# Light experts of a hierarchical MoE decoder layer: gate sums stored in block order, gated rows split on VectorE, list rows copied before the gather, the last expert gated by column halves

## The chip, the cores and the metric

The kernel runs on one core of a Trainium2 chip. The metric is the device time of one execution, in microseconds (us).

## The reference

One decoder layer over 1024 positions of width 1024 in float32. The first half is a mixer (gated linear attention for one group of columns, differential attention for another) with a residual sum. The second half, where the change lies, is a mixture of experts: each token picks one of 4 groups and in it 2 of 8 experts of width 512.

```python
def expert_block(args):
    xb, e = args
    hdn = jax.nn.silu(xb @ w1[e]) * (xb @ w3[e])
    return hdn @ w2[e]
...
out = jnp.zeros((n_tok + 1, d), f32).at[row_tok].add(y.astype(f32) * row_w[:, None])[:n_tok]
```

With 1024 tokens and 32 experts an expert has 64 rows in the mean.

## The kernel before

The part up to about 600 us computes the mixer and the router and puts the 32 experts in order of their row counts. From then on `over_experts` (L2404) runs the experts in that order, as loops written once per engine and unrolled by four: `pe_expert` (L2171), `act_expert` (L2220), `dve_expert` (L2299), `pool_expert` (L2385) and `sp_expert` (L2058). The engines run these streams in order and meet only at semaphores. The first 18 experts are heavy (HEAVY, up to CAP = 96 rows), the other 14 light (up to LIGHT_CAP = 64 rows). A last call with `tail=True` finishes the last expert.

**Weights.** An expert has six chunks of 1 MB: 0 and 1 of w1 (first gate), 2 and 3 of w2 (down), 4 and 5 of w3 (second gate). SP loads them two experts ahead, each when the low part of the same chunk two experts earlier is made (`load_chunk`, L1821; L1817 in the tail). Every chunk is split for fp32r products into a high part (`high`, L2042, a cast on ACT, 2048 columns) and a low part (`low`, L2046, raw minus high on DVE). The parts have three slots, chunk c in slot (c + 1) % 3, so `high` waits until PE has used the chunk three before (`chunk_used`), `low` waits for `high`, and PE waits for `low`.

**One expert on PE.** In the turn of expert e PE takes chunk 0, then brings the hidden part of expert e-1 into transposed form, takes chunk 1, transposes the gathered rows of expert e+1 (L1957), makes a token list (L1911), takes down chunks 2 and 3 of expert e-1, and chunks 4 and 5 of expert e. A heavy product is three matmuls of 512 columns (`product`, L2076 to L2078). A light expert puts the high part of its 64 rows in 64 columns of the weights and the low part in the other 64 (`xT_both`), so `gate` needs two matmuls (L2088, L2089), and the sums of the two halves stand in partitions 0 to 63 and 64 to 127 of PSUM.

**The fold.** These two halves have to be added and transposed. ACT copies each gate's sums to SBUF as `both[m]` (L2242 for the first gate, L2224 for the second, 512 columns), and `fold_mm` (L1968) multiplies them as weights with `fold`, two stacked unit matrices of 64: four matmuls of 64 columns for each gate, each recorded as two instructions, 16 in all. Hidden unit c*4 + k has to land at block k, so the loop reads every fourth column of `both` as weights; the tail, whose down weights are loaded in another row order (L1817), reads whole blocks:

```python
h = both[m][:, j * P:(j + 1) * P] if by_block else both[m].rearrange("p (c k) -> p k c", k=KE)[:, j, :]
last = nc.tensor.matmul(folded[m][:, j, :], h, fold[:], start=True, stop=True)
```

Behind the fold ACT applies SiLU (L2229, `slT`), DVE multiplies (L2294, `hT`), ACT casts the product to its high part (L2232, behind the high part of chunk 3), and DVE makes the low part (L2296), for which the down products wait (`hT_low`). In the tail all of it follows the last gate chunk: copy of 512 columns, both folds, SiLU, product, high, low, then `down_by_half` (L2122). Heavy experts use transposes instead (`h_transposes`, L1964), which read `hd` at the same stride of four.

**Rows in and out.** In each turn POOL first gathers the rows of expert e+3 (L1949, after the token list, L1922, is made), then copies the places and list rows of expert e+4 (`list_rows`, L2381 and L2382, about 1.9 us), for which DVE waits before its `pick` (L1903), and then scatters the rows of expert e-1 (L1990), which ACT has weighted (L2002).

Of the kernel before, what the change touches and what calls it, by code (L numbers as in the profile page):

```python
# [21 lines left out]
F32 = mybir.dt.float32  # L22
# [8 lines left out]
P = 128  # L31
# [1799 lines left out]
def stage_experts(nc, a, s, tools, front):  # L1831
# [44 lines left out]
    pt = four(banks["pt"])  # L1876
    py = [bank[0:CAP] for bank in banks["py"]]
    ph_both = banks["ph"]
    folded = [banks["pt"][:, 256 * m:256 * m + 256].rearrange("p (j x) -> p j x", j=KE) for m in range(2)]
    ident, rows, place, counts, iota = s["ident"], s["slot_rows"], s["place"], s["counts"], s["iota_slot"]  # L1880

# [142 lines left out]
    def slot(c, e=None):  # L2024
        if isinstance(e, int) and e == 0:
            return {0: 1, 1: 2, 4: 0, 5: 3}[c]
        return c + 2 if isinstance(e, int) and e == NE else (c + 1) % 3
# [94 lines left out]
    def down_by_half(pe, e):  # L2122

        for c in (2, 3):
            pe.wait_ge(w_low, number(e, c) + 1)
            for g in range(2):
                for k in range(KE // 2):
                    kx = KE // 2 * (c % 2) + k
                    w = slice(k * D + g * 512, k * D + g * 512 + 512)
                    last = product(py[g][:], hTh[:, kx, :], hTl[:, kx, :], wh[slot(c, e)][:, w],  # L2130
                                   wl[slot(c, e)][:, w], kx == 0, kx == KE - 1)
                if c == 3:
                    last.then_inc(chunk_used, 1)

    def list_tokens(pe, e):

# [34 lines left out]
    def pe_expert(pe, e, r, j, last, light, tail=False):  # L2171
        u = j % 2
        if isinstance(e, int) and e == 0:
            first_gate(pe)
            pe.wait_ge(xT_low, 2)
            gate(pe, 0, 1, u)
            list_weights(pe, 0)
            pe_x(pe, 1, 0, 1)
            list_weights(pe, 1)
            pe_ids(pe, 2, 0)  # L2180
            gate(pe, 0, 4, u)
            pe_ids(pe, 3, 1)
            gate(pe, 0, 5, u)
            return
        if not tail:
            pe.wait_ge(xT_low, 2 * e + 2)
            pe.wait_ge(q.silu, e)
            gate(pe, e, 0, u, light[1])
            if light[0]:
                if isinstance(e, int) and e == HEAVY + 1:  # L2190
                    pe.wait_ge(after["filled"], 13)
                pe.wait_ge(q.hd, e)
                fold_mm(pe, 0)
                fold_mm(pe, 1).then_inc(q.h_mm, 1)
# [24 lines left out]

    def act_expert(act, e, r, j, last, light, tail=False):  # L2220
        u = j % 2
        if light[0]:
            act.wait_ge(chunk_used, number(e - 1, 5) + 1)
            nc.scalar.copy(both[1][:], ph_both[1]).then_inc(q.hd, 1)  # L2224
        if some(e, 1) and not tail:
            high(act, e, r, u, 2)
        if light[0]:
# [5 lines left out]
        elif some(e, 1):  # L2233
            act.wait_ge(q.h_mm, e)
            nc.scalar.copy(hTh[:], pt[:]).then_inc(hT_high, 1)
            high(act, e, r, u, 3)
        if not tail:
            act.wait_ge(chunk_used, number(e, 1) + 1)
            if some(e, 1):
                act.wait_ge(q.hd, e)  # L2240
            if light[1]:
                nc.scalar.copy(both[0][:], ph_both[0]).then_inc(q.silu, 1)  # L2242
            else:
                silu(act, q)
            if some(e, 1):
                high(act, e, r, u, 4)
            if not (last and j == 3):
                act_x(act, e + 1, 1 - u, light[2])
            if some(e, 1):
                high(act, e, r, u, 5)  # L2250
            more = (0, 1) if not (last and j == 3) else ()
        else:
            more = ()
# [35 lines left out]
                nc.vector.tensor_tensor(xTl[u][:, k, :], px[g][:], xTh[u][:, k, :].bitcast(F32),  # L2289
                                        ALU.subtract).then_inc(xT_low, 1)  # L2290

    def turned_hidden(dve, e):
        dve.wait_ge(slT_ready, folds(e))
        nc.vector.tensor_tensor(hT[:], folded[1], slT[:], ALU.mult).then_inc(hT_ready, 1)  # L2294
        dve.wait_ge(hT_high, e)
        nc.vector.tensor_tensor(hTl[:, :, 0:LIGHT_CAP], hT[:], hTh[:, :, 0:LIGHT_CAP].bitcast(F32),  # L2296
                                ALU.subtract).then_inc(hT_low, 1)

    def dve_expert(dve, e, r, j, last, light, tail=False):  # L2299
        u = j % 2  # L2300
        if tail:
            turned_hidden(dve, e)
            low(dve, e, u, 3)
            return
        if light[0]:
# [354 lines left out]
```

## Time and profile before

| | us |
|---|---|
| median of three runs | 1220.89 (1220.45 to 1220.93) |
| profiled execution | 1221.63 |
| its span | 1219.80 |
| PE busy | 1157.8 |
| DVE busy | 882.8 |
| ACT busy | 697.8 |
| POOL busy | 329.5 |

The profile is that of one execution. Engines: PE is TensorE's matmuls, PEld its weight loads, DVE is VectorE, ACT is ScalarE, POOL is GpSimd, SP issues transfers. Times in the trace are counted from the start of the span. PEclk is the TensorE clock that was granted, as a share of full speed; the ends of matmuls are modelled, so starts are the better guide. PE's busy time can't tell how near a stage is to its limit, as an instruction that is loading or streaming slowly counts as busy.

### The profile page before, as it was taken

The numbers are of one execution on the slowest core, as the hardware profiler recorded it, in microseconds if no ns is written. First come the engines' busy times: TensorE is split into PE (matmuls) and PEld (weight loads), VectorE is DVE, ScalarE is ACT, GpSimd is POOL, SyncE is SP. The second block draws the span as 40 slices with busy tenths as digits, with TensorE's granted clock in tenths as the row PEclk, the third lists the DMA queues.
The fourth block names the chain that finished last, engine by engine and source line by source line (L and its number), as shares of the span: only waits on it lengthen the run. The fifth ranks groups of instructions, "written<-read, shape, count | busy, mean of one in ns | idle before, by whom it ended". The sixth has DMA issues, their size and how long they took to land.

```text
span 1219.8 us, 17253 instructions
## 1 busy us (share of the span) xinstructions
PE 1157.8 (95%) x5822; PEld 893.0 (73%) x5823; DVE 882.8 (72%) x1309; ACT 697.8 (57%) x943; POOL 329.5 (27%) x394
## 2 busy tenths in 40 slices
PE   6999999899999899997799999999999999999996
PEld 5868887677776678886567776777777878777774
DVE  4424324666577788886699899999999787888874
ACT  5424203554555633434367777777777676767773
POOL 2212103411111222224524334234243242424111
PEclk9999999999999999999799999999999898999998
DMA  8130210200200543445699999999999999999941
GB/s 315 39 104 1 104 69 1 76 29 27 95 27 19 174 165 134 131 156 207 236 368 389 385 375 395 382 371 390 373 376 386 365 366 341 335 350 340 343 151 18
DMA packets 67326, 271.65 MB, mean 223 GB/s; under 512 B 13172, under 2 KB 19896, under 8 KB 42808
## 3 DMA queue, kind: packets, MB, share of 16 engines
q1 hardware_dynamic: 57000, 245.32, 53.3%
q0 software_dynamic: 6800, 19.14, 6.8%
q10 hardware_dynamic: 3456, 6.29, 1.3%
q8 instruction: 39, 0.64, 0.2%
q14 instruction: 31, 0.25, 0.1%
HBM read 248.44 MB, written 26.48 MB: 225 GB/s over the span
## 4 chain that ended last, share of the span: by engine, by line
PE 80%; DVE 9%; ACT 4%; issue 3%; POOL 2%; DMA 1%; POOLq 0%; ACTq 0%; DVEq 0%
PE main_pm L693 12%; PE main_score L693 6%; PE main_score L2076 5%; PE main_score L2078 5%; PE main_score L2077 5%; PE main_score L1972 4%; DVE main_w_low L2046 3%; PE main_pt L2088 3%; PE main_score L754 3%; PE main_pt L2078 3%; PE main_pt L2076 3%; PE main_pt L2077 3%; PE main_po L2076 3%; PE main_po L2078 3%; PE main_po L2077 3%
## 5 line engine op out<-in xcount | busy, mean ns | idle before, releaser
L2046 DVE TENSOR_TENSOR main_w_low<-w_raw,main_w_high 128x2048 fp32r<-128x2048 f32 x190 | 433.7, 2290 | 39.1 <-ACT main_w_high L2042 38.6
L2042 ACT CAST main_w_high<-w_raw 128x2048 fp32r<-128x2048 f32 x190 | 362.2, 1908 | 72.8 <-PE main_score L2078 56.5
L1949 POOL DMA_INDIRECT main_xg<-xn_dram,main_token x32 | 70.7, 2210 | 359.7 <-DVE main_token L1922 351.8
L2076 PE MATMUL main_score<-main_w_high,main_hT_high 128*96 128x512 f32 x256 | 103.4, 404 | 4.7 <-DVE main_hT_low L2296 4.4
L2078 PE MATMUL main_score<-main_w_high,main_hT_low 128*96 128x512 f32 x256 | 101.2, 396 | 0.0
L2077 PE MATMUL main_score<-main_w_low,main_hT_high 128*96 128x512 f32 x256 | 101.0, 395 | 0.0
L693 PE MATMUL main_pm<-slot_high,xh 128*128 128x512 f32 x208 | 87.7, 422 | 2.1 <-DVE slot_low L1404 2.1
L693 PE MATMUL main_pm<-slot_low,xh 128*128 128x512 f32 x208 | 83.3, 400 | 0.0
L693 PE MATMUL main_pm<-slot_high,xl 128*128 128x512 f32 x208 | 83.0, 399 | 0.0
L1990 POOL DMA_INDIRECT out<-main_y,main_dest x31 | 64.8, 2089 | 57.8 <-ACT main_y L2002 53.4
L1055 ACT ACTIVATE main_prob<-main_score,main_nmax 128x128 f32<-128x128 f32 (+7 forms) x64 | 47.5, 743 | 33.5 <-DVE main_nmax L1463 32.7
L2088 PE MATMUL main_pt<-main_w_high,main_xT_both 128*128 128x512 f32 x112 | 52.6, 470 | 7.9 <-DVE main_w_low L2046 7.9
L2078 PE MATMUL main_po<-main_w_high,main_xT_low 128*96 128x512 f32 x144 | 57.9, 402 | 0.0
L2076 PE MATMUL main_po<-main_w_high,main_xT_high 128*96 128x512 f32 x144 | 57.7, 401 | 0.0
L2077 PE MATMUL main_po<-main_w_low,main_xT_high 128*96 128x512 f32 x144 | 57.6, 400 | 0.0
L2076 PEld LDWEIGHTS main_score<-main_w_high,main_hT_high 128*96 128x96 f32 x256 | 41.8, 163 | 21.2 <-DVE main_hT_low L2296 5.2
L2076 PE MATMUL main_pt<-main_w_high,main_xT_high 128*96 128x512 f32 x140 | 56.3, 402 | 0.0
L2078 PE MATMUL main_pt<-main_w_high,main_xT_low 128*96 128x512 f32 x140 | 55.4, 396 | 0.0
L2381 POOL COPY main_place_of<-place 128x8 f32 x30 | 55.0, 1834 | 1.5 <-POOL slot_rows L546 1.0
L2077 PE MATMUL main_pt<-main_w_low,main_xT_high 128*96 128x512 f32 x140 | 55.0, 393 | 0.0
L2078 PEld LDWEIGHTS main_score<-main_w_high,main_hT_low 128*96 128x96 f32 x256 | 41.7, 163 | 18.1
L2077 PEld LDWEIGHTS main_score<-main_w_low,main_hT_high 128*96 128x96 f32 x256 | 41.8, 163 | 15.8 <-issue 0.2
(359 smaller groups left out, 2627.4 us busy)
## 6 DMA issues: line engine op xcount, KB each, us to landing
w_raw<-in_moe_w SPq DMA_DIRECT2D x192, 1024.0 KB, 13.5
slot_raw<-in_w_in SPq DMA_DIRECT2D x12, 1024.0 KB, 7.6
main_x<-in_x SPq DMA_DIRECT2D x8, 512.0 KB, 11.6
slot_raw<-in_w_out SPq DMA_DIRECT2D x4, 1024.0 KB, 6.9
main_hx<-in_x SPq DMA_DIRECT2D x8, 512.0 KB, 4.0
out<-main_hx SPq DMA_DIRECT2D x8, 512.0 KB, 2.7
xn_dram<-main_xn SPq DMA_DIRECT2D x8, 512.0 KB, 2.9
gr_dram<-main_stage ACTq DMA_DIRECT2D x8, 256.0 KB, 2.0
```

The source lines that it names most:

```text
L693: last = nc.tensor.matmul(bank(i), stationary, moving, start=(k == 0 and n == 0), stop=(k == KD - 1 and n == 2))
L1055: nc.scalar.activation(out, score[comp][:, 0:nk], ACT.Exp, bias=nmax[:, n % 2, comp:comp + 1], accum_out=sums[:, n % 3, comp:comp + 1]).th ...
L1949: nc.gpsimd.indirect_dma_start(xg[u][:], None, s["xn2_dram"], bass.IndirectOffsetOnAxis(token[u][:, 0:1], 0), bounds_check=bound["x"], oob ...
L1972: last = nc.tensor.matmul(folded[m][:, j, :], h, fold[:], start=True, stop=True)
L1990: nc.gpsimd.indirect_dma_start(a["out"].rearrange("b n d -> (b n) d"), bass.IndirectOffsetOnAxis(dest[v][0:slots, 0:1], 0), y[u][0:slots], ...
L2042: nc.scalar.copy(wh[slot(c, e)][:], raw[u][c // 2][:, c % 2, :]).then_inc(w_high, 1)
L2046: nc.vector.tensor_tensor(wl[slot(c, e)][:], raw[u][c // 2][:, c % 2, :], wh[slot(c, e)][:].bitcast(F32), ALU.subtract).then_inc(w_low, 1)
L2076: nc.tensor.matmul(out, x_hi, w_hi, start=start, stop=False)
L2077: nc.tensor.matmul(out, x_hi, w_lo, start=False, stop=False)
L2078: return nc.tensor.matmul(out, x_lo, w_hi, start=False, stop=stop)
L2088: nc.tensor.matmul(ph_both[c // 4], xTb[u][:, kx, :], w_hi[:, w], start=(kx == 0), stop=False)
L2381: nc.gpsimd.tensor_copy(place_of[u][:], place[:, bass.ds(which, 1), :].rearrange("p a t -> p (a t)"))
```

## The change

Five things are changed; loads, loop structure and all other products stay.

1. In the loop ACT writes `both[m]` in block order, reading every fourth column of PSUM (`unfolded`), and `fold_mm` reads whole blocks always.
2. The high part of a light expert's gated rows is made by DVE, right behind the product, and not by ACT.
3. POOL copies the list rows of expert e+4 before the gather of expert e+3.
4. For the last expert PE folds the first gate before chunk 4, takes chunks 4 and 5 in halves of 256 columns into two PSUM banks (`gate_by_half`), and copy, fold, product, high and low part follow for each half.
5. In the tail the first down chunk waits for the first half of the hidden part alone, the second for the other (`down_by_half`).

```diff
-    def fold_mm(pe, m, by_block=False):
+    def fold_mm(pe, m, js=range(KE), out=None):
-        for j in range(KE):
-            h = both[m][:, j * P:(j + 1) * P] if by_block else both[m].rearrange("p (c k) -> p k c", k=KE)[:, j, :]
-            last = nc.tensor.matmul(folded[m][:, j, :], h, fold[:], start=True, stop=True)
+        for i, j in enumerate(js):
+            last = nc.tensor.matmul(folded[m][:, j, :] if out is None else out[:, i, :], both[m][:, j * P:(j + 1) * P],
+                                    fold[:], start=True, stop=True)
         return last
+    def unfolded(act, m):
+        return nc.scalar.copy(both[m].rearrange("p (k c) -> p k c", k=KE),
+                              ph_both[m].rearrange("p (c k) -> p k c", k=KE))
...
+    def gate_by_half(pe, e, u):
+        for c in (4, 5):
             pe.wait_ge(w_low, number(e, c) + 1)
+            w_hi, w_lo = wh[slot(c, e)], wl[slot(c, e)]
+            for half in range(2):
+                out = gated[half][:, 256 * half:256 * half + 256]
+                for k in range(KD // 2):
+                    w = slice(k * DE + 256 * half, k * DE + 256 * half + 256)
+                    kx = KD // 2 * (c % 2) + k
+                    nc.tensor.matmul(out, xTb[u][:, kx, :], w_hi[:, w], start=(kx == 0), stop=False)
+                    last = nc.tensor.matmul(out, xTb[u][:, kx, :], w_lo[:, w], start=False, stop=(kx == KD - 1))
+                if c == 5:
                     last.then_inc(chunk_used, 1)
+    def down_by_half(pe, e, c):
+        pe.wait_ge(hT_low, NE + c - 2)
+        pe.wait_ge(w_low, number(e, c) + 1)
...
-            gate(pe, e, 4, u, light[1])
-            gate(pe, e, 5, u, light[1])
+            if last and j == 3:
+                pe.wait_ge(q.silu, NE)
+                fold_mm(pe, 0).then_inc(q.h_mm, 1)
+                gate_by_half(pe, e, u)
+            else:
+                gate(pe, e, 4, u, light[1])
+                gate(pe, e, 5, u, light[1])
         else:
-            pe.wait_ge(q.hd, e)
-            fold_mm(pe, 0, by_block=True)
-            fold_mm(pe, 1, by_block=True).then_inc(q.h_mm, 1)
-            pe.wait_ge(hT_low, e)
+            for half in range(2):
+                pe.wait_ge(q.hd, NE + half)
+                fold_mm(pe, 1, (2 * half, 2 * half + 1), folded_half[half]).then_inc(q.h_mm, 1)
             pe.wait_ge(q.y_ready, 2 * e - 2)
-            down_by_half(pe, e)
+            for c in (2, 3):
+                down_by_half(pe, e, c)
...
     def act_expert(act, e, r, j, last, light, tail=False):
         u = j % 2
-        if light[0]:
+        if tail:
+            act.wait_ge(q.h_mm, NE)
+            nc.scalar.activation(slT[:], folded[0], ACT.Silu).then_inc(slT_ready, 1)
+            for half in range(2):
+                cols = slice(256 * half, 256 * half + 256)
+                act.wait_ge(chunk_used, number(e - 1, 4 + half) + 1)
+                nc.scalar.copy(both[1][:, cols], gated[half][:, cols]).then_inc(q.hd, 1)
+            high(act, e, r, u, 3)
+        elif light[0]:
             act.wait_ge(chunk_used, number(e - 1, 5) + 1)
-            nc.scalar.copy(both[1][:], ph_both[1]).then_inc(q.hd, 1)
+            unfolded(act, 1).then_inc(q.hd, 1)
...
             high(act, e, r, u, 3)
-            act.wait_ge(hT_ready, folds(e))
-            nc.scalar.copy(hTh[:, :, 0:LIGHT_CAP], hT[:]).then_inc(hT_high, 1)
...
-    def turned_hidden(dve, e):
+    def turned_hidden(dve, e, half=None):
+        k = slice(0, KE) if half is None else slice(2 * half, 2 * half + 2)
+        n = half or 0
+        if half is not None:
+            dve.wait_ge(q.h_mm, NE + 1 + half)
         dve.wait_ge(slT_ready, folds(e))
...
+        dve.wait_ge(hT_ready, folds(e) + n)
+        nc.vector.tensor_copy(hTh[:, k, 0:LIGHT_CAP], hT[:, k, :]).then_inc(hT_high, 1)
...
     def pool_expert(pool, e, r, j, last, light, tail=False):
         u = j % 2
+        if not last:
+            list_rows(pool, e + 4, u)
         if not (tail or (last and j >= 1)):
             pool_gather(pool, e + 3, 1 - u)
-        if not last:
-            list_rows(pool, e + 4, u)
```

## Rows read from the trace of the kernel before

**Rows 1.** the page, busy time of each engine over the span

```profile
PE 1157.8 (95%) x5822; PEld 893.0 (73%) x5823; DVE 882.8 (72%) x1309; ACT 697.8 (57%) x943; POOL 329.5 (27%) x394
```

**Rows 2.** stretches: length, busy of PE, PEld, DVE, ACT, POOL, PEclk, DMA share, GB/s

```profile
640.00:658.70 18.70, 18.66 (x94) 13.34 (x93) 16.93 (x16) 14.13 (x13) 6.49 (x4) 1.00 1.02 382
946.39:966.50 20.11, 19.46 (x90) 15.72 (x89) 16.42 (x16) 14.44 (x15) 6.76 (x5) 0.92 1.00 369
1066.20:1085.23 19.03, 18.45 (x89) 14.75 (x89) 16.30 (x16) 14.37 (x15) 6.29 (x5) 1.00 0.98 350
1010.30:1013.60 3.30, 3.30 (x9) 2.50 (x10) 1.04 (x4) 2.47 (x3) 0.00 (x0) 0.55 1.04 365
1069.70:1071.60 1.90, 1.90 (x9) 1.61 (x10) 0.52 (x2) 1.65 (x2) 0.00 (x0) 1.00 1.05 289
1183.30:1186.80 3.50, 3.50 (x17) 3.50 (x17) 3.16 (x2) 0.83 (x1) 0.00 (x0) 1.00 0.30 56
946.39:1183.30 236.91, 228.88 (x1040) 183.69 (x1040) 193.96 (x173) 173.08 (x169) 67.26 (x41) 0.94 0.93 331
```

**Rows 3.** timeline of PE in one light expert: start, length, engine, line

```profile
1066.20 3.72 PE L1972 MATMUL main_score<-main_fold,main_both 128*128 128x64 f32 x16
1069.72 0.48 PE L2088 MATMUL main_pt<-main_w_high,main_xT_both 128*128 128x512 f32 x1
...
1073.11 0.47 PE L2076 MATMUL main_score<-main_w_high,main_hT_high 128*96 128x512 f32 x1
...
1078.73 0.39 PE L2088 MATMUL main_po<-main_w_high,main_xT_both 128*128 128x512 f32 x1
...
1083.28 0.50 PE L2088 MATMUL main_pt<-main_w_high,main_xT_both 128*128 128x512 f32 x1 [0.44 <-DVE main_w_low L2046]
...
1085.23 1.15 PE L1972 MATMUL main_score<-main_fold,main_both 128*128 128x64 f32 x5
```

**Rows 4.** waits from 620 us on

```profile
PE main_pt L2088 <- DVE main_w_low L2046: 7.9, 13, 0.8
...
DVE main_onehot L1903 <- POOL main_rows_of L2382: 6.6, 27, 0.2
```

**Rows 5.** groups of L1972: 946 to 1187 us, then 1200 to 1203 us

```profile
L1972 PEld LDWEIGHTS main_score<-main_fold,main_both 128*128 128x128 f32 x208 | 49.5, 327 | 0.5
...
L1972 PEld LDWEIGHTS main_score<-main_fold,main_both 128*128 128x128 f32 x16 | 1.9, 192 | 1.1 <-ACT main_both L2224 1.1
```

**Rows 6.** timelines of DVE and of ACT in the same light expert

```profile
1065.31 4.49 DVE L2046 TENSOR_TENSOR main_w_low<-w_raw,main_w_high 128x2048 fp32r<-128x2048 f32 x2
...
1072.46 0.43 DVE L2296 TENSOR_TENSOR main_hT_low<-main_hT,main_hT_high 128x256 fp32r<-128x256 f32 x1 [1.67 <-ACT main_hT_high L2232]
...
1080.88 2.35 DVE L2046 TENSOR_TENSOR main_w_low<-w_raw,main_w_high 128x2048 fp32r<-128x2048 f32 x1 [0.20 <-ACT main_w_high L2042]
...
1072.03 0.40 ACT L2232 CAST main_hT_high<-main_hT 128x256 fp32r<-128x256 f32 x1
...
1078.93 1.92 ACT L2042 CAST main_w_high<-w_raw 128x2048 fp32r<-128x2048 f32 x1 [0.86 <-PE main_score L2078]
...
1083.69 0.58 ACT L2224 COPY main_both<-main_po 128x512 f32<-128x512 f32 x1
```

**Rows 7.** timeline of PEld, transposes of a heavy expert

```profile
687.48 0.56 PEld L1964 LDWEIGHTS main_score<-ident,main_hd 96*128 96x128 f32 x4 [0.48 <-DVE main_hd L1999]
```

**Rows 8.** DMA issues, 640 to 700 us, then 880 to 940 us

```profile
w_raw<-in_moe_w SPq DMA_DIRECT2D x20, 1024.0 KB, 18.0
...
w_raw<-in_moe_w SPq DMA_DIRECT2D x20, 1024.0 KB, 13.6
```

**Rows 9.** timeline of the last expert's end, all engines

```profile
1200.23 2.00 PE L1972 MATMUL main_score<-main_fold,main_both 128*128 128x64 f32 x16 [0.68 <-ACT main_both L2224]
...
1205.25 0.74 PE L2076 MATMUL main_score<-main_w_high,main_hT_high 128*96 128x512 f32 x1 [3.02 <-DVE main_hT_low L2296]
...
1212.17 0.40 PE L2078 MATMUL main_score<-main_w_high,main_hT_low 128*96 128x512 f32 x1
```

More of the change, by code:

```diff
@@ L1878, in stage_experts @@
     ph_both = banks["ph"]
+    gated = [banks["ph"][1], banks["px"][0]]
+    folded_half = [bank[:, 0:2 * LIGHT_CAP].rearrange("p (j x) -> p j x", j=2)
+                   for bank in (banks["px"][1], banks["pid"])]
     folded = [banks["pt"][:, 256 * m:256 * m + 256].rearrange("p (j x) -> p j x", j=KE) for m in range(2)]
@@ L2120, in down @@
         last.then_inc(chunk_used, 1)
-    def down_by_half(pe, e):
-        for c in (2, 3):
+    def gate_by_half(pe, e, u):
+        for c in (4, 5):
             pe.wait_ge(w_low, number(e, c) + 1)
[L2126 to L2132, printed above, removed]
-                    last.then_inc(chunk_used, 1)
+            w_hi, w_lo = wh[slot(c, e)], wl[slot(c, e)]
[7 more added lines that the diff above has]
+                if c == 5:
+                    last.then_inc(chunk_used, 1)
+    def down_by_half(pe, e, c):
+        pe.wait_ge(hT_low, NE + c - 2)
+        pe.wait_ge(w_low, number(e, c) + 1)
+        for g in range(2):
+            for k in range(KE // 2):
+                kx = KE // 2 * (c % 2) + k
+                w = slice(k * D + g * 512, k * D + g * 512 + 512)
+                last = product(py[g][:], hTh[:, kx, :], hTl[:, kx, :], wh[slot(c, e)][:, w],
+                               wl[slot(c, e)][:, w], kx == 0, kx == KE - 1)
+            if c == 3:
+                last.then_inc(chunk_used, 1)
     def list_tokens(pe, e):
@@ L2209, in pe_expert @@
             pe.wait_ge(q.hd, e)
-            gate(pe, e, 4, u, light[1])
-            gate(pe, e, 5, u, light[1])
-        else:
-            pe.wait_ge(q.hd, e)
-            fold_mm(pe, 0, by_block=True)
-            fold_mm(pe, 1, by_block=True).then_inc(q.h_mm, 1)
-            pe.wait_ge(hT_low, e)
+            if last and j == 3:
[5 more added lines that the diff above has]
+                gate(pe, e, 5, u, light[1])
+        else:
+            for half in range(2):
+                pe.wait_ge(q.hd, NE + half)
+                fold_mm(pe, 1, (2 * half, 2 * half + 1), folded_half[half]).then_inc(q.h_mm, 1)
             pe.wait_ge(q.y_ready, 2 * e - 2)
-            down_by_half(pe, e)
+            for c in (2, 3):
+                down_by_half(pe, e, c)
     def act_expert(act, e, r, j, last, light, tail=False):
         u = j % 2
-        if light[0]:
+        if tail:
[7 more added lines that the diff above has]
+        elif light[0]:
             act.wait_ge(chunk_used, number(e - 1, 5) + 1)
-            nc.scalar.copy(both[1][:], ph_both[1]).then_inc(q.hd, 1)
+            unfolded(act, 1).then_inc(q.hd, 1)
         if some(e, 1) and not tail:
             high(act, e, r, u, 2)
-        if light[0]:
+        if light[0] and not tail:
             act.wait_ge(q.h_mm, e)
@@ L2230, in act_expert @@
             high(act, e, r, u, 3)
-            act.wait_ge(hT_ready, folds(e))
-            nc.scalar.copy(hTh[:, :, 0:LIGHT_CAP], hT[:]).then_inc(hT_high, 1)
-        elif some(e, 1):
+        elif some(e, 1) and not tail:
             act.wait_ge(q.h_mm, e)
@@ L2241, in act_expert @@
             if light[1]:
-                nc.scalar.copy(both[0][:], ph_both[0]).then_inc(q.silu, 1)
+                if last and j == 3:
+                    nc.scalar.copy(both[0][:], ph_both[0]).then_inc(q.silu, 1)
+                else:
+                    unfolded(act, 0).then_inc(q.silu, 1)
             else:
@@ L2290, in dve_x @@
                                         ALU.subtract).then_inc(xT_low, 1)
-    def turned_hidden(dve, e):
-        dve.wait_ge(slT_ready, folds(e))
-        nc.vector.tensor_tensor(hT[:], folded[1], slT[:], ALU.mult).then_inc(hT_ready, 1)
-        dve.wait_ge(hT_high, e)
-        nc.vector.tensor_tensor(hTl[:, :, 0:LIGHT_CAP], hT[:], hTh[:, :, 0:LIGHT_CAP].bitcast(F32),
+    def turned_hidden(dve, e, half=None):
[3 more added lines that the diff above has]
+            dve.wait_ge(q.h_mm, NE + 1 + half)
+        dve.wait_ge(slT_ready, folds(e))
+        nc.vector.tensor_tensor(hT[:, k, :], folded[1] if half is None else folded_half[half], slT[:, k, :],
+                                ALU.mult).then_inc(hT_ready, 1)
+        dve.wait_ge(hT_ready, folds(e) + n)
+        nc.vector.tensor_copy(hTh[:, k, 0:LIGHT_CAP], hT[:, k, :]).then_inc(hT_high, 1)
+        dve.wait_ge(hT_high, e + n)
+        nc.vector.tensor_tensor(hTl[:, k, 0:LIGHT_CAP], hT[:, k, :], hTh[:, k, 0:LIGHT_CAP].bitcast(F32),
                                 ALU.subtract).then_inc(hT_low, 1)
@@ L2301, in dve_expert @@
         if tail:
-            turned_hidden(dve, e)
+            for half in range(2):
+                turned_hidden(dve, e, half)
             low(dve, e, u, 3)
```

## The prediction

> **What bounds the kernel now.** I read the page first: PE is busy for 95% of the span [rows 1]. That share says little, because it mixes stages, so I cut the expert stage up. The edit touches only the light experts, which run from 946 us on. The table of stretches [rows 2] gives each of them one row. A light expert takes 19.03 us where PEclk is 1.00 and 20.11 us where it is 0.92. All other engines have room there: DVE 16.30 us, ACT 14.37 us of 19.03. The whole loop over twelve periods, from the fold of expert 18 to that of expert 30, takes 236.91 us; with four periods of about 19.0 and eight of about 20.1 this adds up.
>
> The timeline of one fast light expert [rows 3] shows where PE's time goes, counted from the start of the fold (1066.20 is zero). The fold lasts to 3.52, the second gate chunk, the turned x and the lists to 6.91, the two down chunks to 12.53, gate chunks 4 and 5 follow, the next expert's chunk 0 starts at 17.08 and ends at 19.03. Chunk 0 waits for its low part; the list of waits has this wait 13 times, 7.9 us in all [rows 4]. Its chain is in the timelines of ACT and DVE [rows 6]: down chunk 3 frees the slot at 12.53, ACT's high part starts at 12.73 (1078.93, 1.92 us), DVE's low part at 14.68 (1080.88, 2.35 us), and PE goes on at 17.08. So the period is a ring: fold 3.52, second chunk with x and lists 3.39, down 5.62, high and low 4.55, chunk 0 1.95: 19.03. All of the fold stands in this ring; gate chunks 4 and 5 don't, they lie beside high and low.
>
> The slow periods differ in one place. PE's nine instructions behind the fold took 3.30 us at a granted clock of 0.55 of full speed, the same nine 1.90 us at 1.00 [rows 2]: the clock had fallen to its lower level, 1.2 GHz, after 3.5 us of fold. The period grows by 20.1 - 19.0 = 1.1 us of the 1.4, the rest is slack.
>
> **The change, part by part.** *Block order.* The fold multiplies read their weights at a stride of four elements now. A load takes 327 ns in the loop, and 192 ns in the tail, where the same 16 instructions read whole blocks [rows 5]. On PE the 16 took 3.72 us with a stride [rows 3], 2.00 us without [rows 9]. Start to start, 3.52 us become (2.00 - 0.25)/15 x 16 = 1.87 us: 1.65 us less per expert, all in the ring. Twelve periods give 12 x 1.65 = 19.8 us.
>
> *ACT's copies.* The reordering moves into ACT's two copies, which now read PSUM at that stride. No row has that. The lower bound is today's 0.58 us [rows 6]; the upper one the pace at which PE loads at this stride: 3.52/16 = 0.22 us per 128 columns, so 0.88 us for 512, plus 0.2 to start, 1.1 us. A gain is excluded, as no element fewer is read. I take 0.58, the row of the same engine. ACT has 17.4 - 14.0 us of idle time, and the copy of chunk 5 ends at 18.07 of 19.03 [rows 6], 0.96 before the fold wants it. In the new period it would end 0.96 before again, since weighted sums and high parts hang on the same ring. At 1.1 us it still fits; the following high part slips by 0.5 and the hidden part by up to 0.3 us, at most 3.6 us over twelve.
>
> The Trainium skill, "SBUF — State Buffer", section "Door 1: The DMA port swizzle", speaks against this part: PSUM is read in lines of two fp32 values, and a non-contiguous pattern significantly slows matmuls. It gives no figure for ScalarE. By it the cost would lie at the 1.1 us end or past it.
>
> *High part on DVE.* ACT loses a 0.40 us cast at 1072.03, which stood behind a 1.9 us high part; DVE had waited 1.67 us for it [rows 6]. DVE gains about 0.43 us, the length of its neighbour of the same size (bounds 0.2 and 0.6), and stands at 16.3 + 0.43 = 16.7 us of a 17.4 us period. Behind the fold DVE is in chunk 2's low part until 3.60 (1065.31 + 4.49), then product, high and low part end at about 4.9. PE wants the hidden part at 6.91 - 1.65 = 5.26. So this edit is what lets the ring shrink: with ACT's cast it would be late by some 1.4 us. Cover 0.35 us; if it is gone, the down chunks start that much later.
>
> *List rows ahead of the gather.* DVE's wait for them falls away, 6.6 us in 27 [rows 4]. It lies beside the ring: chunk 1's low part starts 0.25 us earlier. On POOL, the gather and its DMA, then the scatter behind it no longer stand behind 1.9 us of copying; both transfers start earlier, none of them is waited for. Worth 0 alone.
>
> *Clock.* With the fold at 1.9 us and not 3.5, PE's slow stretch is half as long. A heavy expert, which never folds, ran at 1.00 [rows 2]. I take all eight dips as gone: 8 x 1.1 = 9 us.
>
> *The end.* Now: fold of expert 30 at 1183.30, last down product at 1212.17 [rows 9], 28.9 us. New, from that fold: fold 1.87, second chunk to 3.7, down from 4.7 (hidden part; no x here) to 10.3, the folded first gate 0.95 to 11.2, then 32 products of 256 columns. These cost at least 0.117 us (the fold's pace) and at most 0.23 (a full one's, 1.83/8): 3.7 to 7.4 us. I take 3.7, half the columns, half the time: 14.95, the first half 0.95 earlier. That half's copy is hidden, its fold 0.45 us, its product, high and low part three short DVE steps of 0.25 and waits: 16.45. First down chunk to 19.3. The last low part: ACT's copy of the second half to 15.55, high 1.9, DVE 2.3 behind the second half's three steps: 19.8. Second down chunk to 22.5. So 6.4 us saved; 3.6 us less if the products are slow, 1.5 less if the clock falls again as it did here (6.92 us from the first down product to the last [rows 9], where 5.4 is usual, 5.62 - 0.23). I take 6.
>
> **Sum.** The profiled execution took 1221.63 us (span 1219.80). 1221.63 - 19.8 - 9 - 6 = 1186.8. The median shown is 0.74 lower, 1220.89, so I forecast 1186.5 with a little kept back.
>
> **Rivals.** *Dips stay.* The chunk 5 to chunk 0 pause on PE and the fold together are still 2.7 us of thin work, and in the tail the clock fell after 2.0 us of fold and 3.0 of idle. For it: a dip here comes with no other visible cause. Against: heavy experts. Eight dips: 1195.5; twelve: 1200.
>
> *Stride was not it.* The transposes of heavy experts also load at a stride of four, and four took 0.56 us, 0.11 to 0.14 each [rows 7], no slower than contiguous folds. The tail's fold ran with DVE idle and DMA quiet. Then the loop's folds stay at 3.5, and only the end gains: 1220.9 - 6 = 1215. Against: expert 30's fold at 1183.30 had a DMA share of 0.30 and still filled its 3.5 us [rows 2], so a quiet DMA doesn't make it fast. In the skill's "SBUF — State Buffer", same section, a stride up to four fp32 is free; by that rule the fold would gain nothing. The 327 against 192 ns speak the other way.
>
> *Another engine binds.* DMA: in the heavy stage it was full (1.02, 382 GB/s), and landing fell from 18.0 to 13.6 us in 240 us [rows 8], 0.34 us per expert of 18.70, so a heavy expert's traffic needs 18.36 us. A light one scatters 32 rows fewer, some 0.5 us: about 17.8 against 17.4. A chunk is asked for about 30 us before it is needed and lands in 14, so twelve times 0.4 us is covered. If DMA, or ACT's slow copy with DVE, sets 18 us instead: 7 us more, 1194.
>
> *Slower than before.* ACT's strided copy as the bound: high 0, weighted sums, high 1, copy lie in a row from 10.9 to 16.1 + x, and then comes the fold. The period reaches today's mean of 19.7, and the end's 6 us are also eaten, when 16.1 + x = 20.2, x = 4.1 us: seven times the contiguous copy, four times my upper bound. Then 1221 and up, at 5 us 1233.
>
> **How the numbers follow.** Forecast as summed 0.58 (own range 1182 to 1191), dips stay in part or all 0.24, another engine 0.08, stride not it 0.05, changes cancel to within 0.2% 0.02, slower 0.03. 0.2%, 2.4 us, is about what a measurement of this kernel can tell. Faster 0.95, same 0.02, slower 0.03. The range takes in the dips and the third case: 1182 to 1201.
>
> **What would show it.** L1972's loads near 190 ns and its matmuls near 2 us per expert; light periods of 17.4 us; PEclk 1.00 in the loop; the strided copies at 0.6 and not 1.1; the last down product 22 to 24 us behind the last full fold. Loads still at 327, periods over 18.5, or a copy over 1.5 us would prove me wrong.

## The result, and the profile after

The changed kernel took 1172.54 us (median of four runs, 1171.87 to 1173.47) against 1220.91, a ratio of 0.9605 with a 95% interval of 0.9589 to 0.9622. That is 48 us less, where 34 were forecast and the range went down to 1182. The profiled execution took 1173.08 us, its span 1171.3.

The page's first part answers to [rows 1]:

```profile
PE 1116.4 (95%) x5838; PEld 860.8 (73%) x5839; DVE 882.4 (75%) x1326; ACT 692.8 (59%) x930; POOL 335.6 (29%) x394
```

Busy shares hardly moved; as before, they tell nothing of where 48 us went. The table of stretches answers to [rows 2] (columns as there): the same 18.70 us of the heavy stage as there (its period is shorter now, see below), one light period from fold to fold, and the loop's light stage.

```profile
640.00:658.70 18.70, 18.70 (x95) 13.59 (x94) 17.12 (x16) 14.42 (x13) 6.09 (x5) 1.00 1.02 384
973.13:990.03 16.90, 16.31 (x91) 12.80 (x90) 16.40 (x17) 14.07 (x14) 7.98 (x5) 1.00 1.02 388
939.10:1142.00 202.90, 195.44 (x1046) 153.28 (x1044) 194.78 (x185) 169.25 (x157) 77.80 (x40) 1.00 1.01 386
```

The light period is 16.90 us, PEclk is 1.00 for the whole light stage, where it was 0.94, and DVE is busy for 16.40 of the 16.90. The same period in PE's timeline answers to [rows 3]:

```profile
972.97 1.89 PE L1974 MATMUL main_score<-main_fold,main_both 128*128 128x64 f32 x16
974.67 0.48 PE L2095 MATMUL main_pt<-main_w_high,main_xT_both 128*128 128x512 f32 x1
...
977.82 0.46 PE L2083 MATMUL main_score<-main_w_high,main_hT_high 128*96 128x512 f32 x1
...
983.43 0.39 PE L2095 MATMUL main_po<-main_w_high,main_xT_both 128*128 128x512 f32 x1
...
987.92 0.50 PE L2095 MATMUL main_pt<-main_w_high,main_xT_both 128*128 128x512 f32 x1 [0.59 <-DVE main_w_low L2053]
...
989.87 1.33 PE L1974 MATMUL main_score<-main_fold,main_both 128*128 128x64 f32 x11
```

From the fold's start at zero, the fold lasts to 1.70 (3.52 before), the down chunks start at 4.85 (6.91) and end at 10.46 (12.53), chunk 0 starts at 14.95 (17.08) and ends at 16.90 (19.03). DVE and ACT in that period, as in [rows 6]:

```profile
976.97 0.42 DVE L2340 TENSOR_TENSOR main_hT_low<-main_hT,main_hT_high 128x256 fp32r<-128x256 f32 x1
...
985.58 2.29 DVE L2053 TENSOR_TENSOR main_w_low<-w_raw,main_w_high 128x2048 fp32r<-128x2048 f32 x1 [0.39 <-ACT main_w_high L2049]
...
976.98 0.58 ACT L1979 COPY main_both<-main_pt 128x512 f32<-128x512 f32 x1
...
983.63 1.91 ACT L2049 CAST main_w_high<-w_raw 128x2048 fp32r<-128x2048 f32 x1 [0.86 <-PE main_score L2085]
```

The low part of the hidden rows ends at 977.39, 0.43 us before PE takes it at 977.82. The copy that reads PSUM at a stride of four took 0.58 us at 976.98, no more than the contiguous one in [rows 6]. From high (983.63) over low (985.58) to chunk 0 (987.92), the chain of the ring is unchanged. POOL's two copies of list rows take 4.5 us in this period, where they took 1.9 before, as they now run beside DVE's low parts; they end at 976.35, and `pick`, which wants them, comes at 987.79, so this costs nothing.

The fold's weight loads over all light experts (shortest, median and longest in ns), which answer to [rows 5]:

```profile
L1974 PEld LDWEIGHTS main_score<-main_fold,main_both x220: 187/192/193, 938.9 to 1156.5; 128*128 128x128 f32 x110
```

The light stage begins earlier, too. The first full fold starts at 939.12 and not at 946.23. The transposes of the hidden part run once per heavy expert; first and last start of the 72 of them, before and after:

```profile
L1964 PE MATMUL main_score<-ident,main_hd x72: 283/284/360, 612.7 to 930.8; 96*128 96x96 f32 x72
```

```profile
L1967 PE MATMUL main_score<-ident,main_hd x72: 247/283/360, 610.7 to 923.8; 96*128 96x96 f32 x72
```

Between the first and the last lie 17 heavy periods: 318.1 us before, 313.0 after, 18.71 and 18.41 us each. So 5 us were gained in a stage in which the forecast saw nothing to gain. The remaining 2 us lie ahead of the first transpose (612.7 to 610.7); with the runs below they stay unsettled. What changed in the heavy ring is in DVE's timeline, first before, around the transposes of [rows 7]:

```profile
683.66 0.96 DVE L1903 TENSOR_TENSOR main_onehot<-iota_slot,main_place_of 128x768 bf16<-128x768 f32 x1 [0.24 <-POOL main_rows_of L2382]
684.54 2.28 DVE L2046 TENSOR_TENSOR main_w_low<-w_raw,main_w_high 128x2048 fp32r<-128x2048 f32 x1
686.74 0.68 DVE L1999 TENSOR_TENSOR main_hd<-main_po,main_sl 96x512 f32<-96x512 f32 x1
```

And after, one expert later:

```profile
698.77 0.95 DVE L1906 TENSOR_TENSOR main_onehot<-iota_slot,main_place_of 128x768 bf16<-128x768 f32 x1
699.64 2.29 DVE L2053 TENSOR_TENSOR main_w_low<-w_raw,main_w_high 128x2048 fp32r<-128x2048 f32 x1
701.84 0.68 DVE L2006 TENSOR_TENSOR main_hd<-main_po,main_sl 96x512 f32<-96x512 f32 x1
```

The token pick (L1903, now L1906) has lost its wait of 0.24 us for POOL. Behind it stand, on the same engine, chunk 1's low part and the hidden product (L1999), and for that product PE's transposes waited in every heavy expert. The list of waits of the heavy stage (600 to 935 us; us in total, times, longest), before and after:

```profile
PEld main_score L1964 <- DVE main_hd L1999: 11.6, 18, 2.4
```

```profile
PEld main_score L1967 <- DVE main_hd L2006: 2.8, 6, 1.1
```

The wait came 18 times before, once per heavy expert, and comes six times now.

The end, PE from the last full fold on, answers to [rows 9]:

```profile
1141.59 1.89 PE L1974 MATMUL main_score<-main_fold,main_both 128*128 128x64 f32 x16
...
1152.37 0.36 PE L2139 MATMUL main_po<-main_w_high,main_xT_both 128*128 128x256 f32 x1
...
1156.28 0.56 PE L1974 MATMUL main_score<-main_fold,main_both 128*128 128x64 f32 x4
...
1157.86 0.45 PE L2083 MATMUL main_score<-main_w_high,main_hT_high 128*96 128x512 f32 x1 [0.29 <-issue]
...
1161.12 0.44 PE L2083 MATMUL main_score<-main_w_high,main_hT_high 128*96 128x512 f32 x1 [0.26 <-DVE main_w_low L2053]
...
1163.71 0.40 PE L2085 MATMUL main_score<-main_w_high,main_hT_low 128*96 128x512 f32 x1
```

From the last full fold to the last down product 22.1 us pass, 28.9 before; the forecast was 22.5. The second down chunk waited 0.26 us for its low part. The products of 256 columns started every 0.12 us, the lower of the two bounds.

Last, the landing of weight chunks, that is the median time from the issue of a transfer to its end in us (the last number of a row), in three stretches (640 to 700, 880 to 940, 1060 to 1110 us), as in [rows 8]:

```profile
w_raw<-in_moe_w SPq DMA_DIRECT2D x20, 1024.0 KB, 18.6
...
w_raw<-in_moe_w SPq DMA_DIRECT2D x20, 1024.0 KB, 19.0
...
w_raw<-in_moe_w SPq DMA_DIRECT2D x18, 1024.0 KB, 27.6
```

In the kernel before it was 7.7 us in the third stretch.

The gain by place, in the two profiled executions: 7.1 us ahead of the first full fold, 237.1 - 202.5 = 34.6 in twelve light periods, 6.8 behind the last full fold. That is the whole difference of the two spans, 48.5 us.

### The profile page after: what moved, and what is told of

The parts are those of the page before. It is cut to its first block, busy times and chain, and to the rows that moved or that the text cites. A ratio compares the mean times of both kernels' runs of the same rounds, so it can differ in the third digit from the quotient of the medians.

```text
span 1171.3 us, 17264 instructions
## 1 busy us (share of the span) xinstructions
PE 1116.4 (95%) x5838; PEld 860.8 (73%) x5839; DVE 882.4 (75%) x1326; ACT 692.8 (59%) x930; POOL 335.6 (29%) x394
## 4 chain that ended last, share of the span: by engine, by line
PE 80%; DVE 10%; ACT 5%; POOL 2%; issue 2%; DMA 1%; ACTq 0%; POOLq 0%; DVEq 0%
PE main_pm L693 13%; PE main_score L693 7%; PE main_score L2083 5%; PE main_score L2085 5%; PE main_score L2084 5%; DVE main_w_low L2053 4%; PE main_score L754 3%; PE main_pt L2085 3%; PE main_po L2085 3%; PE main_pt L2083 3%; PE main_po L2083 3%; PE main_pt L2084 3%; PE main_po L2084 3%; ACT main_w_high L2049 2%; PE main_pt L2095 2%; PE main_po L777 2%
## 5 line engine op out<-in xcount | busy, mean ns | idle before, releaser
L1952 POOL DMA_INDIRECT main_xg<-xn_dram,main_token x32 | 75.2, 2349 | 280.9 <-DVE main_token L1925 269.8
L1997 POOL DMA_INDIRECT out<-main_y,main_dest x31 | 50.1, 1616 | 87.2 <-ACT main_y L2009 60.2
L2426 POOL COPY main_place_of<-place 128x8 f32 x30 | 59.3, 1978 | 1.4 <-POOL slot_rows L546 1.0
L2095 PE MATMUL main_pt<-main_w_high,main_xT_both 128*128 128x512 f32 x112 | 46.4, 414 | 8.1 <-DVE main_w_low L2053 8.1
L1257 POOL TENSOR_SCALAR main_o_rs<-main_o_ss 128x1 f32<-128x1 f32 x32 | 10.3, 321 | 152.6 <-ACT main_o_sq L1071 152.3
```

The source lines that it names most:

```text
L1952: nc.gpsimd.indirect_dma_start(xg[u][:], None, s["xn2_dram"], bass.IndirectOffsetOnAxis(token[u][:, 0:1], 0), bounds_check=bound["x"], oob ...
L1997: nc.gpsimd.indirect_dma_start(a["out"].rearrange("b n d -> (b n) d"), bass.IndirectOffsetOnAxis(dest[v][0:slots, 0:1], 0), y[u][0:slots], ...
L2095: nc.tensor.matmul(ph_both[c // 4], xTb[u][:, kx, :], w_hi[:, w], start=(kx == 0), stop=False)
L2426: nc.gpsimd.tensor_copy(place_of[u][:], place[:, bass.ds(which, 1), :].rearrange("p a t -> p (a t)"))
```

## The experiments

Ratios are against the kernel before on the same chip, whose median was 1219.28 us for the first four kernels, 1220.50 for the next four and 1219.45 for the last three.

### The list rows alone

```diff
     def pool_expert(pool, e, r, j, last, light, tail=False):
+        if not last:
+            list_rows(pool, e + 4, u)
         if not (tail or (last and j >= 1)):
             pool_gather(pool, e + 3, 1 - u)
-        if not last:
-            list_rows(pool, e + 4, u)
```

> The kernel before, with the list rows copied ahead of the gather and nothing else. Theory (pick in the ring): in a heavy expert the token pick of DVE stands in the chain that sets the period, since the hidden product and the transposes wait behind it; taking its wait away shortens a heavy period from 18.70 to 18.40 us and the start of the expert stage by 1.5 us, and leaves the light periods at 19.0 and 20.1. So 1220.9 - 6.8 = 1214 us. Rival (the 7 us ahead of the light stage belong to other edits, or to transfers that start earlier): this edit alone is worth nothing, 1221, as the prediction had it.

Measured: 1212.09 us, ratio 0.9957 (0.9940 to 0.9973), 7.2 us less than its 1219.28. The transposes of the heavy experts:

```profile
L1964 PE MATMUL main_score<-ident,main_hd x72: 246/283/360, 608.1 to 921.1; 96*128 96x96 f32 x72
```

313.0 us for the 17 periods, as in the changed kernel, and the transposes wait for the hidden product six times, not 18. The theory holds: moving two small copies on POOL shortens a heavy period by 0.30 us, 5 us in all; the rest of the 7.2 us lies ahead of the first transpose or within the noise of some 2 us. The periods of the light stage stayed between 18.9 and 20.3 us, seven of twelve of them long, with the lower clock.

### The block order alone

```diff
-            h = both[m][:, j * P:(j + 1) * P] if by_block else both[m].rearrange("p (c k) -> p k c", k=KE)[:, j, :]
+            h = both[m][:, j * P:(j + 1) * P]
...
-            nc.scalar.copy(both[1][:], ph_both[1]).then_inc(q.hd, 1)
+            unfolded(act, 1).then_inc(q.hd, 1)
```

The first gate's copy is changed likewise; in the tail the copies stay plain.

> The kernel before, with the block order in the loop alone; ACT still casts the high part behind the high part of chunk 3. Theory (nearly independent): the fold takes 1.7 and not 3.5 us, the dips of the clock go, and the cast on ACT, which starts as soon as SiLU starts earlier, makes the hidden part late by 0.3 us at most: periods of 17.0 to 17.4, 1220.9 - 12 x 2.5 = 1190 us. Rival (as on record): with the cast on ACT the hidden part comes 1.4 us late, periods of 18.4 to 18.6, 1205 us. Third case (the dips stay): four or five periods in ten longer by 1.1, 1200 us.

Measured: 1188.11 us, ratio 0.9750 (0.9734 to 0.9766), 31.2 us less. The twelve periods took 206.2 us, 17.18 each, without a dip (PEclk 1.00 over all of them). PE and ACT in one of them:

```profile
996.67 1.89 PE L1972 MATMUL main_score<-main_fold,main_both 128*128 128x64 f32 x16
...
1001.17 0.48 PE L1911 MATMUL main_pm<-main_rows_of,main_onehot 128*96 128x6 bf16 x8
1001.76 0.47 PE L2080 MATMUL main_score<-main_w_high,main_hT_high 128*96 128x512 f32 x1
```

```profile
998.60 0.39 ACT L2236 ACTIVATE main_slT<-main_score 128x256 f32<-128x256 f32 x1 [1.08 <-PE main_score L1972]
...
1000.68 0.40 ACT L2239 CAST main_hT_high<-main_hT 128x256 fp32r<-128x256 f32 x1
```

ACT's cast comes at 1000.68, 4.0 us behind the start of the fold at 996.67, where it was 5.8 us behind before [rows 3, 6]: SiLU comes earlier with the fold, and the high part of chunk 3 and the cast move with it. The down products start at 1001.76 and could have started some 0.25 us earlier, judging by the pause behind the lists (0.59 us here, 0.34 in the changed kernel). The 1.4 us of the prediction were wrong: I had moved PE's need by 1.65 us and left ACT's queue where it was.

### The cast on DVE alone

```diff
             high(act, e, r, u, 3)
-            act.wait_ge(hT_ready, folds(e))
-            nc.scalar.copy(hTh[:, :, 0:LIGHT_CAP], hT[:]).then_inc(hT_high, 1)
...
+        dve.wait_ge(hT_ready, folds(e))
+        nc.vector.tensor_copy(hTh[:, :, 0:LIGHT_CAP], hT[:]).then_inc(hT_high, 1)
```

> The kernel before, with the high part of the gated rows made by DVE alone, the folds still strided. Theory: only the wait for the hidden part goes, 0.26 us in each fast period and about 1 us each at the last two hand-overs; dips stay as they are: 1216 us. Rival (the dips of the clock come from the wait behind the lists and not from the length of the fold): the dips go too, 1207 us.

Measured: 1219.96 us, ratio 1.0002 (0.9989 to 1.0015): nothing. The light stage (columns of [rows 2]):

```profile
944.00:1183.00 239.00, 230.72 (x1042) 185.56 (x1041) 199.32 (x185) 169.78 (x157) 68.31 (x41) 0.93 0.93 327
```

Here the granted clock is 0.93 on average. The fast periods did fall from 19.0 to 18.4 or 18.7, but ten of twelve were long ones, and not eight. Neither of my cases had that: the wait went and more periods had a dip. The rival is out, since the dips did not go.

### All but the new end

The block order, the cast on DVE and the list rows as in the three diffs above, the last expert's end as before.

> Block order, cast on DVE and list rows first, but the last expert's end as before: one fold of both gates behind the last gate chunk, no halves. Theory (the end is independent): 1172.5 + 6.7 = 1179 us, heavy periods 18.4, light ones 16.9, PEclk 1.00 in the loop. Rival: the halves free banks or slots for the loop too, and its periods grow over 17.1, 1182 us or more.

Measured: 1174.11 us, ratio 0.9640 (0.9624 to 0.9656), 45.2 us less than its 1219.28. The three edits alone give 7.2 + 31.2 + 0 = 38.4 us, together 45.2. The 6.8 us between them, with a noise of some 4 us, are what the cast and the list rows are worth on top once the fold is short: the runs below give 3.0 us for the cast, and 1.4 us for the list rows in the light stage. Against the changed kernel's 0.9597 to 0.9605 the new end is worth 0.0035 to 0.0043, 4 to 5 us with a noise of some 3, where 6.7 were expected. PE at this end:

```profile
1152.51 2.00 PE L1972 MATMUL main_score<-main_fold,main_both 128*128 128x64 f32 x16 [0.68 <-ACT main_both L2229]
1156.23 0.74 PE L2080 MATMUL main_score<-main_w_high,main_hT_high 128*96 128x512 f32 x1 [1.72 <-DVE main_hT_low L2306]
```

The down products start at 1156.23 with a longer first one (0.74 us), as before [rows 9]. From the last full fold, at 1137.98, to the last down product it takes 26.3 us, 28.9 before and 22.1 changed: 2.6 us of what I had put down to the new end come from the short fold and the cast on DVE, 4.2 from the halves.

Of those 4.2 us only 2.0 are work that overlaps better (the first down product comes 18.25 us behind the last full fold here, 16.27 in the changed kernel). The other 2.2 are clock. The down products of this kernel, and those of the changed one:

```profile
1156.23:1164.66 8.43, 8.43 (x24) 5.37 (x24) 2.29 (x1) 1.17 (x2) 0.00 (x0) 0.66 0.01 2
```

```profile
1157.86:1164.11 6.25, 5.99 (x24) 3.68 (x24) 2.91 (x4) 1.48 (x2) 0.00 (x0) 1.00 0.18 33
```

Here the granted clock was 0.50, the lower of its two levels (1.2 and 2.4 GHz), for the first 5.7 us, after PE had folded for 2.0 us and then waited for 1.7. In the changed kernel, where PE has gate products up to the fold and waits 0.3 us, it stayed at 1.00. All five kernels with the old end have this dip, for 3 to 6 us.

### The changed kernel again, two parts undone, one doubled

Undone are, in this order, the list rows' place and the cast on DVE, which then casts for the last expert alone; the third diff does the folds twice over.

```diff
-        if not last:
-            list_rows(pool, e + 4, u)
         if not (tail or (last and j >= 1)):
             pool_gather(pool, e + 3, 1 - u)
+        if not last:
+            list_rows(pool, e + 4, u)
```

```diff
             high(act, e, r, u, 3)
+            act.wait_ge(hT_ready, folds(e))
+            nc.scalar.copy(hTh[:, :, 0:LIGHT_CAP], hT[:]).then_inc(hT_high, 1)
```

```diff
                 fold_mm(pe, 0)
+                fold_mm(pe, 1)
+                fold_mm(pe, 0)
                 fold_mm(pe, 1).then_inc(q.h_mm, 1)
```

> The changed kernel as it is, to stand beside the runs of this call on one chip. Theory and rival alike: 0.960 of the kernel before, 1171 to 1173 us, first full fold at about 936 to 939 us, periods of 16.9 us.

Measured: 1171.71 us, ratio 0.9597 (0.9575 to 0.9619).

> The changed kernel with the list rows copied behind the gather again. Theory (pick in the ring of the heavy experts): heavy periods go back to 18.70, the first full fold comes 7 us later, and the light periods, whose ring passes by pick, stay at 16.9: 7 us over the changed kernel run beside it. Rival (in the light stage DVE is so near its limit that a wait of 0.25 us counts there too): light periods grow by 0.25 as well, 10 us over it.

Measured: 1179.30 us, ratio 0.9669 (0.9652 to 0.9686), 7.6 us over the changed kernel. Heavy transposes, and the light stage:

```profile
L1967 PE MATMUL main_score<-ident,main_hd x72: 283/286/360, 610.3 to 928.4; 96*128 96x96 f32 x72
...
943.90:1131.00 187.10, 181.85 (x961) 140.94 (x960) 180.27 (x174) 154.66 (x144) 62.04 (x40) 1.00 1.02 389
```

318.1 us for 17 heavy periods again, 5.0 of the 7.6 us. The eleven light periods in the second row took 17.0 us each, 0.1 to 0.15 more than 16.9, 1.4 us in twelve, so the rival has a part of it. In the period from 1011.97 us on, DVE's wait of 0.25 us before `pick` ends the low part of the hidden rows 4.72 us behind the fold's start, 4.42 in the changed kernel's period from 1006.77 on. That eats the cover, and the down chunks start 0.10 us later (4.95 and 4.85). Besides, chunk 0's low part takes 2.35 us with POOL's copies beside it, and 2.29 without.

> The changed kernel with the loop's high part of the gated rows cast by ACT again. Theory (from the run with block order alone, periods 17.18 against 16.90): 0.28 us per period, 3.4 us over the changed kernel. Rival (as on record, 1.4 us late): 17 us over it.

Measured: 1174.67 us, ratio 0.9628 (0.9609 to 0.9646), 3.0 us over the changed kernel. The theory's 3.4 fit, the prediction's 17 don't.

> The changed kernel with the loop's two folds done twice over, with the same result: 32 contiguous instructions, 3.4 us, about as long as the strided fold took. Theory (the dips came from the length of that stretch): periods of 16.9 + 1.7 = 18.6 us, and on top dips as before, 1.1 us in about two of three periods: 12 x 1.7 + 8 x 1.1 = 29 us over the changed kernel. Rival (they came from the slow strided loads, and a dense fold is work enough for the clock): PEclk stays 1.00, 12 x 1.7 = 20 us over it.

Measured: 1194.43 us, ratio 0.9785 (0.9766 to 0.9805), 22.7 us over the changed kernel. Ten light periods, then one of them:

```profile
939.00:1126.00 187.00, 180.11 (x1041) 145.79 (x1041) 166.06 (x160) 140.55 (x131) 74.88 (x38) 1.00 1.01 378
957.90:976.60 18.70, 18.01 (x107) 14.61 (x105) 16.68 (x17) 14.08 (x14) 7.97 (x5) 1.00 1.01 385
```

The 32 fold instructions take 3.5 us, the length of the strided fold, and PEclk stays at 1.00. My theory is refuted: the length of that stretch alone did not bring the clock down.

### The folds strided again

```diff
-            last = nc.tensor.matmul(folded[m][:, j, :] if out is None else out[:, i, :], both[m][:, j * P:(j + 1) * P],
+            h = both[m].rearrange("p (c k) -> p k c", k=KE)[:, j, :] if strided else both[m][:, j * P:(j + 1) * P]
+            last = nc.tensor.matmul(folded[m][:, j, :] if out is None else out[:, i, :], h,
                                     fold[:], start=True, stop=True)
...
-            unfolded(act, 1).then_inc(q.hd, 1)
+            nc.scalar.copy(both[1][:], ph_both[1]).then_inc(q.hd, 1)
```

The first gate's copy and fold are changed likewise in the first of the two kernels, and not in the second.

> The changed kernel with the loop's folds strided again (ACT copies in column order), all other parts kept. Theory (slow strided loads are what lets the clock fall, since the dense fold of the same length did not): periods of 16.9 + 1.8 = 18.7 us, and dips in half or more of them, 1.1 to 1.4 us each: 28 to 32 us over the changed kernel, 1200 to 1204 us. Rival (the dips belonged to the rest of the kernel before, such as the wait for ACT's cast): no dips, 22 us over it, 1194 us, as with the folds done twice.

Measured: 1206.39 us, ratio 0.9882 (0.9863 to 0.9901), some 35 us over the changed kernel. The light stage and one long period:

```profile
939.70:1157.00 217.30, 209.82 (x963) 169.13 (x962) 182.70 (x174) 155.75 (x144) 78.06 (x39) 0.94 0.99 358
958.65:978.60 19.95, 19.30 (x89) 15.47 (x89) 16.58 (x17) 13.99 (x14) 8.25 (x5) 0.91 1.01 379
```

PEclk is back at 0.94, with nine of twelve periods long (19.9 to 20.3 us) and three of 18.7 to 18.8. All other edits are in this kernel, so the strided fold alone brings the dips, and a contiguous one of equal length doesn't. Two things differ between those two stretches of 3.5 us, though: the stride of the loads, and that PE does 16 fold instructions in one and 32 in the other. No run separates them, for instance by 16 contiguous ones spread over 3.5 us. The twelve periods took 237.0 us, 34.5 more than the changed kernel's: 12 x 1.85 = 22.2 us of it are fold, the other 12 go with the dips.

> The changed kernel with the second gate's fold strided and the first one's in block order. Theory (load time goes by the stride alone): the two folds take 2.6 us, periods of 17.8 us, 11 us over the changed kernel. If any strided stretch lets the clock fall, PEclk is under 1.00 in part of the periods and it is 15 us or more; if it takes the whole 3.5 us of it, PEclk stays 1.00.

Measured: 1185.09 us, ratio 0.9719 (0.9705 to 0.9734). Eleven light periods:

```profile
938.50:1135.00 196.50, 189.26 (x964) 151.35 (x963) 182.13 (x174) 155.07 (x144) 76.19 (x39) 1.00 1.01 388
```

The two folds take 2.7 us, the periods 17.8 us, and PEclk is 1.00: with half of the fold strided, the strided loads cost their own time and no clock. The twelve periods took 213.8 us, 11.3 over the changed kernel's, as expected. The medians are 13.4 apart, on different chips, and where the other 2 us come from stays open.

### Chunk 0's low part by halves

```diff
+            if halves and k == KD // 4:
+                pe.wait_ge(w_low, number(e, c) + 1)
...
         if not (last and j == 3):
-            low(dve, e + 1, 1 - u, 0)
+            for half in range(2):
+                low_half(dve, e + 1, 1 - u, 0, half)
```

PE waits for the first half on a semaphore of its own (`w_half`, its lines are not shown).

> The changed kernel with chunk 0's low part made in two halves and PE starting on the first (heavy and light experts). Theory (the weight traffic is next): the ring loses about 1.1 us, but DVE is busy for 16.4 of 16.9 us in a light period and transfers take 18.4 us per heavy and 17.7 per light expert, and the backlog ahead of need is nearly used up; so ACT's high parts begin to wait for DMA and the gain is 0 to 4 us. Rival (the ring through chunk 0 is the only bound): 0.9 us in each of 30 periods, 27 us under the changed kernel.

Measured: 1169.91 us, ratio 0.9598 (0.9584 to 0.9612): no gain that can be told from the changed kernel's 0.9597 and 0.9605. One wait and the light stage:

```profile
ACT main_w_high L2050 <- DMA w_raw<-in_moe_w: 2.5, 4, 1.6
...
940.00:1100.00 160.00, 157.94 (x844) 124.16 (x842) 157.27 (x166) 133.92 (x124) 69.90 (x36) 1.00 1.02 391
```

ACT now waits for DMA four times, 2.5 us in all; the changed kernel's list of waits has no such line. DVE is busy for 157.3 of 160.0 us, and PE for 157.9. Its light periods took 16.8 us, against 16.9, and its 17 heavy ones 313.2 us, against 313.0. So the ring through chunk 0 is not the only bound. In the light stage DVE, at 98%, and the transfers stand close behind it; which of the two binds there, and what binds the heavy stage, this run does not tell.

## Why the prediction was wrong

The direction, the place of the ring and most of its terms were right; the time was below the range. Against the sum for the profiled execution, 1186.8 us, the changed kernel's 1173.08 is 13.7 lower: 7.1 us ahead of the light stage, where the sum had nothing, 5.8 in the light ring and 0.8 at the end. The range ended 4.5 us under the forecast, so each of the first two would alone have left it. Point by point:

- **The light ring.** "Period = fold, second chunk with x and lists, down, high and low, chunk 0" held within its own terms: 1.70 + 3.15 + 5.61 + 4.49 + 1.95 = 16.90. Forecast was 17.38. Mis-sized were the fold (1.70, not 1.87; I had scaled the tail's fold, which starts behind a wait, and the loop's runs on) and the second term (3.15, not 3.39): the 3.39 held a wait of about 0.25 us for ACT's cast, which I had read as work. With the 0.06 of high and low (chunk 0's low part, 2.29 us and not 2.35, now that POOL's copies don't run beside it) it is 0.48 us a period, 5.8 us in twelve.
- **The list rows, "worth 0 alone".** This step failed. It priced the edit in the light ring, where pick lies beside it but for 0.1 to 0.15 us, and never looked at the heavy one, where pick stands in it: 0.30 us in each of 17 periods, 5 of the 7.1 us. The row for it stood among mine: the transposes of [rows 7] carry a wait of 0.48 us for the hidden product. I used that row for the stride and passed over its bracket. Alone the edit gave 7.2 us, and without it the changed kernel took 7.6 more.
- **The clock.** All dips went, as forecast, 9 us. The reason given, "PE's slow stretch is half as long", is not the one: the doubled fold lasted 3.5 us, the full length, and had no dip. Dips came only where the whole fold was strided. So the number was right by luck, and whether the stride counts or the fewer products in the same time stays open.
- **ACT's strided copies.** 0.58 us, the lower bound. The line of the Trainium skill ("SBUF — State Buffer", "Door 1: The DMA port swizzle") on non-contiguous PSUM patterns speaks of matmuls; for ScalarE's copies this trace shows no cost.
- **"Stride was not it".** The loads went to 192 ns in the loop. The same section of the Trainium skill lets fp32 stride by up to four for free; the fold's loads, 329 against 192 ns, disagree, so the measurement decides. It also says that each access that crosses to a new 16-byte line pays a penalty, which at a stride of four fp32 would be every access, and that fits the fold. But the transposes with the same stride [rows 7] were not as slow, before or after (their loads took 217 and 218 ns in the median), so neither sentence fits both: the cost falls on these fp32 products, and why is open.
- **The high part on DVE.** The size was right in sum (0.30 us on DVE at 976.64 to 976.94, within the bounds of 0.2 and 0.6) and wrong in meaning: not 1.4 but 0.25 to 0.3 us per period hung on it.
- **The end.** 6.8 us measured, 6 taken. The halves account for 4.2 of them, and 2.2 of those are a dip that did not come. The sum took it as gone and gave no reason (it priced its return at 1.5 us), so this term is in part luck.
- **DMA.** The estimate of 17.8 us per light expert fits: at periods of 16.9 the landing rose from 19.0 to 27.6 us in about ten experts, 0.8 each, so an expert's transfers took some 17.7. Of the cover of about 30 us little was left when the stage ended.

What stays open: the other 2 of the 7.1 us, ahead of the first heavy transpose. That transpose began between 607 and 611 us in the runs with the list rows first, and between 610 and 613 in those with them last, so the two overlap.

## What to carry to other kernels

Cost an edit on every loop that runs it, and in each find the ring that sets the period first; a move that is free in one stage may sit in the ring of another. When a step is pulled earlier, move the other engines' queues with it before you call one of them late, and read each row's bracket for what it waits for. And as rings get shorter, watch the landing times: they tell how much of the transfers' cover is left.

## What the runs showed of the hardware

- fp32 weight loads of 128 columns for products of 64 columns took 329 ns at a stride of four elements and 192 ns without; start to start 0.22 and 0.11 us. The loads of transposes at that stride took 217 ns (96 rows, four in 0.56 us).
- In four kernels a fold of 3.5 us, all of it with such strided loads, was followed by the lower granted clock in seven to ten of twelve periods. With 32 contiguous instructions in 3.5 us, or with half of the 16 strided in 2.7 us, it was so in none of twelve.
- In the last expert's end the granted clock was 0.50 for the first 3 to 6 us of down products in all five kernels with the old end, behind 2.0 us of fold and a wait of 1.7 or 3.0 us; with gate products up to the fold and a wait of 0.3 us it stayed at 1.00.
- ACT reads 128x512 floats from PSUM at a stride of four in 0.58 us, as without a stride.
- DVE's low part of 2048 columns took 2.29 us, and 2.35 us with POOL's copies of list rows beside it.
- fp32r products of 256 columns with new weights each start every 0.12 us, half of the 0.23 us for 512.
